# Second up product with stationary weights: both halves of all tokens move side by side, and three engines make the squared relu

## Chip, cores and metric

The kernel runs on one core of a Trainium2 chip. The metric is the device time of one execution in microseconds (us). TensorE multiplies, VectorE and ScalarE work on rows from its banks (PSUM) and from on-chip memory (SBUF), GpSimd works on SBUF, and the SyncE queue starts the loads from HBM. Every engine runs its own program strictly in order, and semaphores order the engines against one another.

## The reference, cut to what matters

256 tokens of width 1024 pass two blocks. The change lies in the last part of the second one, an MLP with a squared relu:

```python
u = rms_norm_2(x, g_mlp_pre) @ w_up        # 256 x 1024 @ 1024 x 4096
u = jnp.square(jax.nn.relu(u))
x = x + rms_norm_2(u @ w_down, g_mlp_post) # 256 x 4096 @ 4096 x 1024
```

## The kernel before

All large products are made from halves. ScalarE rounds an fp32 operand to the reduced type in which TensorE is fast (the high part), VectorE makes the rest (the low part, the operand less its high part), and TensorE adds up high x high, high x low and low x high in a bank (`three_products`, L1536 to L1541). Weights and activations are both split so.

The weights come in units of 128 x 2048 (1 MB), loaded by SyncE into eight places. `make_high` (ScalarE) and `make_low` (VectorE) split one unit each; there are four places for high parts, so a unit waits until the unit four before it is used up. In the up product `mu` the gain of the norm is folded into the weights, so that a unit is split in four pieces of 128 x 512 (L484, L504); the down product `md` splits a unit at once (L477, L495). ScalarE signals a unit once, behind its last piece, and VectorE starts on it then.

`mu` has 8 slabs of 512 of the 4096 columns, two units each (the first and the second 512 of the 1024 contracted values). For each slab, `split_use` makes 48 matmuls: the tokens are stationary, 128 by 128, and 512 columns of weights move through; the two tiles of 128 tokens have a bank each, and two slabs alternate between four banks `G`. The result has tokens on the partitions. ScalarE scales it by the norm's rstd, a column with one value for each token, and takes the relu (`relu`, L1473); VectorE squares it (`relu_squared`, L2979); TensorE turns the squares with transposes into banks `T` while it works on the slab behind (`squared_turn`); ScalarE copies the high part out of `T` (`hidden_high`, L1141) and VectorE makes the low part (`hidden_low`, L2352). So the squares stand with the 4096 values on the partitions, 32 chunks of 128, as `md` needs them for its stationary operand.

In each round s of the loop over slabs, ScalarE and VectorE first split the two units of slab s+1 (`make_slab`; in round 7 the first two of `md`), then take the turned squares of slab s-1, then scale and square slab s. `md` (`split_down`) has 16 units of two chunks. In its first unit it makes the products of one token tile, the last transposes, and then those of the other tile. `rest_high` and `rest_low` split its other units after the loop.

Of the kernel before, what the change touches and what calls it, by code (L numbers as in the profile page):

```python
# [16 lines left out]
P = 128  # L17
S = 256
# [197 lines left out]
def build(nc, t, out):  # L216
    with ExitStack() as ctx:
# [3 lines left out]
        def sem(name):  # L221
            return ctx.enter_context(nc.semaphore(name))
# [20 lines left out]
        dense_high = place(HIGH * UNIT, RAW * UNIT, "dense_high", F32R)  # L243
        xT_lo_all = place(KD * S, 12 * UNIT, "xT_lo_all", F32R)
        turned_all = place(4 * S, 13 * UNIT, "turned_all", F32)
        gate_parts_all = place(KD * 2 * HEADS + P, 13 * UNIT + 4 * S, "gate_parts_all", F32R)
# [69 lines left out]
        post_gain1 = work[:, 0, PROJ:PROJ + D]  # L316
        post_gain2 = ring[:, 6 * SLAB + KD * S:6 * SLAB + KD * S + D]

# [69 lines left out]
        sines_exp_ready = sem("sines_exp_ready")  # L388
        relu_ready = sem("relu_ready")
        relu2_ready = sem("relu2_ready")  # L390
# [39 lines left out]
        def consumed(eng, n):  # L430

            ph = phase_of(n)
            u = n - ph.first
            if ph in (ao, fo, bo, po, md):
                if u < ph.units - 1:
                    eng.wait_ge(ph.used, u + 1)
                else:
                    eng.wait_ge(down_full, ph.downs + 4)
            elif u % 2:
                eng.wait_ge(ph.full, 2 * (u // 2 + 1))  # L440
            else:
                eng.wait_ge(ph.half_used, u // 2 + 1)
# [415 lines left out]
        def _(pool):  # L858
# [169 lines left out]
            pool.wait_ge(rows_cleared, 1)  # L1028
            nc.gpsimd.memset(hT[0:AUG, 24:32, :], 0.0).then_inc(rows_cleared, 1)


        @block.scalar
        def _(act):
# [22 lines left out]

            def high_turn(tf, g, c, gc):

# [396 lines left out]
            post_norm_squares(12, 0)  # L1455
            high_turn(turned2, base, 0, None)
            post_norm_squares(12, 1, lambda: make_high(act, mu.first + 2))
            square(0, 16 + 2)
            high_turn(turned2, base + 2, 1, None)
            make_high(act, mu.first + 3)  # L1460
# [4 lines left out]

            def relu(s, c):
                n = 2 * s + c
                act.wait_ge(mu.full, n + 1)
                if s:
                    act.wait_ge(relu2_ready, n - 1)  # L1470
                else:
                    act.wait_ge(rstd_ready, 10 + c + 1)
                nc.scalar.activation(xn[:, c, 0:BANK], G[2 * (s % 2) + c][:, :], ACT.Relu, scale=rstd[:, c:c + 1]).then_inc(mu.done, 1)  # L1473

            for s in range(mu.slabs):
                if s:
                    make_slab(make_high, act, mu, s + 1, md)
                for c in range(NT):
                    if s:
                        hidden_high(turned2, base + 2 * (s - 1) + c, s - 1, c, 4)  # L1480
                for c in range(NT):
                    relu(s, c)
# [8 lines left out]
        def _(pe):  # L1491
# [56 lines left out]

            def split_first(ph, tc, base, other_tile, late=0):

# [657 lines left out]

            split_first(mu, tc, base, second_tile2, late=1)
            base += 4  # L2210
            for s in range(1, mu.slabs):
                split_use(mu, s, lambda: slab_before(squared_turn, s, base))
            pe.wait_ge(mu.done, 2 * mu.slabs - 2)

            def last_squared():
                pe.wait_ge(mu.done, 2 * mu.slabs)
                slab_before(squared_turn, mu.slabs, base)

            split_down(md, *hidden_parts, chunk_ready(base, 4, tc), last=4, free=mu.slabs % 2, turns=last_squared)


        @block.vector
        def _(dve):
# [51 lines left out]

            def low_turn(tc, c, gc, between=None):

# [684 lines left out]

            post_norm(1, post_gain1, 0)
            low_turn(tc, 0, None)
            make_low(dve, mu.first + 1)
            post_norm(1, post_gain1, 1)
            low_turn(tc, 1, None)
            make_low(dve, mu.first + 2)
# [4 lines left out]

            def relu_squared(s, c, base):
                n = 2 * s + c
                dve.wait_ge(mu.done, n + 1)
                if s:
                    dve.wait_ge(tf, base + n - 1)
                V.tensor_tensor(xn[:, c, BANK:2 * BANK], xn[:, c, 0:BANK], xn[:, c, 0:BANK], ALU.mult).then_inc(relu2_ready, 1)  # L2979

            for s in range(mu.slabs):
                if s:
                    make_slab(make_low, dve, mu, s + 1, md)
                for c in range(NT):
                    if s:
                        hidden_low(tc, s - 1, c, 4)
                for c in range(NT):
                    relu_squared(s, c, base)
            for c in range(NT):
                hidden_low(tc, mu.slabs - 1, c, 4)  # L2990
            rest_low(md)
# [25 lines left out]
```

## Time and profile before

| | |
|---|---|
| median of 3 runs | 1855.09 us (1854.59 to 1855.69) |
| profiled execution | 1854.42 us, span 1852.8 us |
| TensorE busy | 1837.0 us, 99% of the span |
| VectorE, ScalarE, GpSimd busy | 75%, 65%, 9% |
| chain that ended last | TensorE 96%, VectorE 2%, ScalarE 1% |
| slabs 1 to 7 of the up product | 1675.62 to 1758.13 us, 11.79 us each |

The span is the time from the first to the last recorded instruction; the 1.6 us between it and the device time lie around it. Matmuls are pipelined: each is shown with its whole duration, so they overlap in the record, and the pace is the distance between their starts.

### The profile page before, as it was taken

How to read it: one execution, taken by the hardware profiler on the slowest of the kernel's cores; microseconds unless marked ns; L12 is line 12 of the kernel's file. 1: busy time of each engine (PE TensorE's matmuls, PEld its weight loads, DVE VectorE, ACT ScalarE, POOL GpSimd, SP SyncE). 2: the span in 40 equal slices, each digit the busy share in tenths (PEclk: the TensorE clock that was granted, in tenths of full speed). 3: DMA queues.
4: the chain of work that ended last, by engine and by line, in shares of the span. 5: the costliest groups of instructions: out<-in, count | busy, mean ns of one | idle time of the engine just before them, and what ended most of it. 6: DMA issues, size and time to landing. Idle time of an engine off the chain costs nothing.

```text
span 1852.8 us, 25653 instructions
## 1 busy us (share of the span) xinstructions
PE 1837.0 (99%) x8824; PEld 1544.9 (83%) x8824; DVE 1394.9 (75%) x1561; ACT 1200.1 (65%) x1346; POOL 159.2 (9%) x185
## 2 busy tenths in 40 slices
PE   9999999999999999999999999999999999999998
PEld 8998888888888888888888888888888887878887
DVE  6666476646676888888888888988888997587653
ACT  5544365437765777677676777777777676666542
POOL 3000000004404400000000000000000321000000
PEclk9999999999999999999999999999999999999999
DMA  9656655554439999999999999999999973345550
GB/s 294 185 184 206 195 184 188 182 186 155 137 125 336 338 396 395 394 394 393 395 395 396 394 393 384 381 386 367 394 375 371 394 295 106 134 148 166 177 196 30
DMA packets 237863, 516.19 MB, mean 279 GB/s; under 512 B 15260, under 2 KB 55312, under 8 KB 237792
## 3 DMA queue, kind: packets, MB, share of 16 engines
q1 hardware_dynamic: 232304, 499.70, 75.3%
q0 software_dynamic: 5184, 14.51, 2.2%
q10 hardware_dynamic: 304, 1.05, 0.2%
q8 instruction: 41, 0.67, 0.1%
q14 instruction: 30, 0.25, 0.0%
HBM read 506.78 MB, written 8.42 MB: 278 GB/s over the span
## 4 chain that ended last, share of the span: by engine, by line
PE 96%; DVE 2%; ACT 1%; issue 0%; ACTq 0%; DVEq 0%; POOL 0%; POOLq 0%
PE G L1539 24%; PE G L1541 24%; PE G L1540 24%; PE SM L1541 5%; PE SM L1539 5%; PE SM L1540 5%; PE T L1499 3%; PE T L1952 1%; PE SM L1727 1%; PE G L1818 1%; DVE e_low L724 1%; PE SM L1836 0%; PE SM L2096 0%; PE G L1937 0%; PE G L2065 0%
## 5 line engine op out<-in xcount | busy, mean ns | idle before, releaser
L724 DVE TENSOR_TENSOR e_low<-e_arrived,e_high 128x2048 fp32r<-128x2048 f32 (+1 forms) x346 | 758.9, 2247 | 86.9 <-ACT e_high L716 86.9
L716 ACT CAST e_high<-e_arrived 128x2048 fp32r<-128x2048 f32 x338 | 624.4, 1914 | 4.8 <-PE SM L1541 4.8
L1539 PE MATMUL G<-e_high,work_r 128*128 128x512 f32 x896 | 353.8, 395 | 1.0 <-DVE e_low L724 0.7
L1541 PE MATMUL G<-e_high,work_r 128*128 128x512 f32 x896 | 349.4, 390 | 0.0
L1540 PE MATMUL G<-e_low,work_r 128*128 128x512 f32 x896 | 348.6, 389 | 0.0
L1539 PE MATMUL G<-dense_high,xT_hi_all 128*128 128x512 f32 (+1 forms) x760 | 294.2, 387 | 1.7 <-ACT work_all L1125 0.7
L1541 PE MATMUL G<-dense_high,xT_lo_all 128*128 128x512 f32 (+1 forms) x760 | 283.3, 373 | 0.0
L1540 PE MATMUL G<-dense_low,xT_hi_all 128*128 128x512 f32 (+1 forms) x760 | 282.5, 372 | 0.0
L495 DVE TENSOR_TENSOR dense_low<-dense_raw,dense_high 128x2048 fp32r<-128x2048 f32 (+1 forms) x73 | 147.9, 2055 | 89.1 <-ACT dense_high L477 88.1
L1541 PEld LDWEIGHTS G<-e_high,work_r 128*128 128x128 f32 x896 | 168.1, 188 | 35.9
L1539 PEld LDWEIGHTS G<-e_high,work_r 128*128 128x128 f32 x896 | 168.3, 188 | 35.2 <-DVE e_low L724 1.6
L1540 PEld LDWEIGHTS G<-e_low,work_r 128*128 128x128 f32 x896 | 168.4, 188 | 33.6
L504 DVE SCALAR_TENSOR_TENSOR dense_low<-dense_raw,gains,dense_high 128x512 fp32r<-128x512 f32 x216 | 148.7, 752 | 49.5 <-ACT dense_high L484 49.5
L1539 PE MATMUL SM<-e_high,work_r 128*128 128x512 f32 x448 | 175.8, 392 | 0.0
L477 ACT CAST dense_high<-dense_raw 128x2048 fp32r<-128x2048 f32 (+1 forms) x73 | 123.0, 1722 | 81.0 <-PE G L1541 81.0
L1541 PE MATMUL SM<-e_high,work_r 128*128 128x512 f32 x448 | 174.6, 390 | 0.0
L1540 PE MATMUL SM<-e_low,work_r 128*128 128x512 f32 x448 | 174.4, 389 | 0.0
L1539 PEld LDWEIGHTS G<-dense_high,xT_hi_all 128*128 128x128 f32 x760 | 143.0, 188 | 20.9 <-issue 1.6
L1541 PEld LDWEIGHTS G<-dense_high,xT_lo_all 128*128 128x128 f32 x760 | 142.6, 188 | 21.0
L1540 PEld LDWEIGHTS G<-dense_low,xT_hi_all 128*128 128x128 f32 x760 | 143.1, 188 | 17.9
L1539 PE MATMUL G<-dense_high,hT_hi_all 128*128 128x512 f32 x376 | 147.7, 393 | 0.8 <-ACT work_all L1219 0.8
L1540 PE MATMUL G<-dense_low,hT_hi_all 128*128 128x512 f32 x376 | 146.3, 389 | 0.0
(380 smaller groups left out, 2078.9 us busy)
## 6 DMA issues: line engine op xcount, KB each, us to landing
e_arrived<-in_m_w_in_dram SPq DMA_DIRECT2D x448, 512.0 KB, 8.6
e_arrived<-in_m_w_out_dram SPq DMA_DIRECT2D x224, 512.0 KB, 8.6
dense_raw<-in_a_w_in_dram SPq DMA_DIRECT2D x32, 768.0 KB, 6.0
dense_raw<-in_f_w_in_dram SPq DMA_DIRECT2D x44, 512.0 KB, 4.6
dense_raw<-in_w_up_dram SPq DMA_DIRECT2D x16, 1024.0 KB, 5.2
dense_raw<-in_w_down_dram SPq DMA_DIRECT2D x16, 1024.0 KB, 4.9
dense_raw<-in_a_w_out_dram SPq DMA_DIRECT2D x12, 1024.0 KB, 5.0
dense_raw<-in_f_w_out_dram SPq DMA_DIRECT2D x11, 1024.0 KB, 4.9
```

The source lines that it names most:

```text
L477: ins = nc.scalar.copy(high_place(n)[:, 0:4 * w], unit_place(n, dense_raw)[:, 0:4 * w])
L495: ins = nc.vector.tensor_tensor(unit_place(n, dense_low)[:, 0:4 * w], unit_place(n, dense_raw)[:, 0:4 * w], high_place(n)[:, 0:4 * w].bitc ...
L504: ins = nc.vector.scalar_tensor_tensor(out=low, in0=raw, scalar=by[kk], in1=high.bitcast(F32), op0=ALU.mult, op1=ALU.subtract)
L716: nc.scalar.copy(e_hi_unit(n), e_raw(n, e_arrived)).then_inc(e_hi, 1)
L724: ins = nc.vector.tensor_tensor(e_raw(n, e_low)[:, at], e_raw(n, e_arrived)[:, at], e_hi_unit(n)[:, at].bitcast(F32), ALU.subtract)
L1499: ins = nc.tensor.transpose(T[par(g)][0:k, at:at + P], src, ident[:, :])
L1539: nc.tensor.matmul(bank, x_hi, w_hi, start=start, stop=False)
L1540: nc.tensor.matmul(bank, x_hi, w_lo, start=False, stop=False)
L1541: return nc.tensor.matmul(bank, x_lo, w_hi, start=False, stop=stop)
L1727: nc.tensor.matmul(SM[c][:, 0:GDIM], work[:, c, A_HALF + s * P:A_HALF + (s + 1) * P], work[:, c, s * GDIM:(s + 1) * GDIM], start=True, sto ...
L1818: nc.tensor.matmul(G[2 + u % 2][:, 0:nk], hT[0:AUG, HEADS + hd, q * P:(q + 1) * P], hT[0:AUG, hd, 0:nk], start=True, stop=True).then_inc(a ...
L1952: ins = nc.tensor.transpose(T[p % 2][:, n * P:(n + 1) * P], e_hid[:, p % 2, n * P:(n + 1) * P], ident[:, :])
```

## The change

From its second slab on, the up product has the weights stationary. The halves of the activations of all 256 tokens lie side by side (`x_halves_all`, for each of the 8 contracted blocks 256 columns of high and 256 of low parts). With 128 x 128 of high weights stationary, one matmul moves all 512 columns into a bank: its left half gets high x high, its right half high x low. With the low weights stationary, a second matmul moves the 256 high columns and adds into the left half. A bank so holds 128 of the 4096 values for all 256 tokens, already with the values on the partitions; a slab fills four banks, and eight banks alternate. The transposes of slabs 1 to 7 go, and the relu's scale by rstd becomes a product with rows: one matmul of ones with a diagonal matrix of rstd spreads rstd over the partitions (`rstd_row`).

A chunk then passes three engines: ScalarE copies the right half out of the bank (`copy_side`), VectorE adds it to the left half (`sum_chunk`), GpSimd takes the relu and multiplies by `rstd_row`, ScalarE squares and makes the high part (`square_chunk`), and VectorE makes the low part (`lower_chunk`). Slab 0 stays as it was. `post_gain2`, the gain loaded on ScalarE's queue, has another place. The diff without declarations:

```diff
+            pool.wait_ge(side_ready, 3)
+            for m in range(4 * (mu.slabs - 1)):
+                pool.wait_ge(mu.done, 2 + m + 1)
+                steps.then(nc.gpsimd.tensor_scalar(up_sum[:, m % 4, :], up_sum[:, m % 4, :], 0.0, 1.0, ALU.max, ALU.mult))
+                nc.gpsimd.tensor_tensor(up_sum[:, m % 4, :], up_sum[:, m % 4, :], rstd_row, ALU.mult).then_inc(relu2_ready, 1)
...
+            def copy_side(m):
...
+                act.wait_ge(mu.full, 2 + m + 1)
+                if m >= 2:
+                    act.wait_ge(mu.done, 2 + m - 1)
+                nc.scalar.copy(up_side[:, m % 2, :], bank[:, S:2 * S]).then_inc(side_ready, 1)
+
+            def square_chunk(m):
+
+                act.wait_ge(relu2_ready, 2 + m + 1)
+                steps.then(nc.scalar.activation(up_square[:, m % 4, :], up_sum[:, m % 4, :], ACT.Square))
+                nc.scalar.copy(hT_hi[:, 4 + m, :], up_square[:, m % 4, :]).then_inc(split_copied, 1)
+
             for c in range(NT):
-                hidden_high(turned2, base + 2 * (mu.slabs - 1) + c, mu.slabs - 1, c, 4)
+                relu(c)
+            for s in range(1, mu.slabs):
+                make_slab(make_high, act, mu, s + 1, md)
+                if s == 1:
+                    for c in range(NT):
+                        hidden_high(turned2, base + c, 0, c, 4)
+                    act.wait_ge(side_ready, 2)
+                    nc.scalar.copy(rstd_row, G[0][:, 0:S]).then_inc(side_ready, 1)
+                for j in range(4):
+                    m = 4 * (s - 1) + j
+                    copy_side(m)
+                    if m:
+                        square_chunk(m - 1)
+            square_chunk(4 * (mu.slabs - 1) - 1)
...
+            def up_slab(s, between):
+
+                banks = up_banks(s)
+                for part in range(2):
+                    n = mu.first + 2 * s + part
+                    split_ready(n)
+                    w_hi, w_lo = high_place(n), low_place(n)
+                    for j in range(4):
...
+                        elif part == 0 and s > 2:
+                            pe.wait_ge(mu.done, 2 + 4 * (s - 3) + j + 1)
+                        for kk in range(4):
+                            k = 4 * part + kk
+                            at = slice(kk * BANK + j * P, kk * BANK + (j + 1) * P)
+                            both = lambda stop: nc.tensor.matmul(banks[j][:, :], w_hi[:, at], x_halves_all[:, 2 * k * S:2 * (k + 1) * S],
+                                                                 start=(k == 0), stop=stop)
+                            if k < KD - 1:
+                                both(False)
+                            ins = nc.tensor.matmul(banks[j][:, 0:S], w_lo[:, at], mu_hi[:, k, :], start=False, stop=False)
+                            if k == KD - 1:
+                                ins = both(True)
+                        if part:
+                            ins.then_inc(mu.full, 1)
...
+            def first_squared():
+
+                slab_before(squared_turn, 1, base)
+                pe.wait_ge(side_ready, 1)
+                nc.tensor.matmul(G[0][:, 0:S], ones[:, :], rstd_diag, start=True, stop=True).then_inc(side_ready, 1)
...
+            pe.wait_ge(mu.done, 2 + 4 * (mu.slabs - 2))
+
+            def last_free():
+                pe.wait_ge(mu.done, 2 + 4 * (mu.slabs - 2) + 2)
...
+            split_down(md, *hidden_parts, up_ready, last=4, free=0, turns=last_free)
...
+            for c in range(NT):
+                ins = V.tensor_scalar(rstd_diag[:, c * P:(c + 1) * P], ident[:, :], rstd[:, c:c + 1], None, ALU.mult)
+            ins.then_inc(side_ready, 1)
...
+            def sum_chunk(m):
...
+                dve.wait_ge(side_ready, 3 + m + 1)
+                V.tensor_tensor(up_sum[:, j, :], bank[:, 0:S], up_side[:, m % 2, :], ALU.add).then_inc(mu.done, 1)
+
+            def lower_chunk(m):
+
+                high_parts[0] += 1
+                dve.wait_ge(split_copied, high_parts[0])
+                V.tensor_tensor(hT_lo[:, 4 + m, :], up_square[:, m % 4, :], hT_hi[:, 4 + m, :].bitcast(F32), ALU.subtract
+                                ).then_inc(tc[0], 1)
+
             for c in range(NT):
-                hidden_low(tc, mu.slabs - 1, c, 4)
+                relu_squared(c)
+            for s in range(1, mu.slabs):
+                make_slab(make_low, dve, mu, s + 1, md)
+                if s == 1:
+                    for c in range(NT):
+                        hidden_low(tc, 0, c, 4)
+                for j in range(4):
+                    m = 4 * (s - 1) + j
+                    if m >= 2:
+                        lower_chunk(m - 2)
+                    sum_chunk(m)
+            for m in (4 * (mu.slabs - 1) - 2, 4 * (mu.slabs - 1) - 1):
+                lower_chunk(m)
```

## Rows read from the trace of the kernel before

**Rows 1.** Page, 40 slices of the span: granted TensorE clock in tenths.

```profile
PEclk9999999999999999999999999999999999999999
```

**Rows 2.** Waits of TensorE, 1660 us to the end.

```profile
PE G L1539 <- DVE xT_lo_all L2286: 0.2, 1, 0.2
```

**Rows 3.** Windows of slabs 1 and 7: busy us (instructions), clock, DMA share, GB/s.

```profile
1675.62:1687.40 11.78, 11.78 (x57) 9.84 (x56) 9.12 (x22) 8.22 (x15) 0.00 (x0) 1.00 0.70 246
...
1746.34:1758.13 11.79, 11.79 (x58) 9.84 (x57) 7.07 (x6) 6.06 (x6) 0.00 (x0) 1.00 0.49 180
```

**Rows 4.** Timeline of TensorE in slab 3: start us, us, operation, tiles, count.

```profile
1699.64 0.39 PE L1541 MATMUL G<-dense_high,xT_lo_all 128*128 128x512 f32 x1
...
1704.40 0.39 PE L1541 MATMUL G<-dense_high,xT_lo_all 128*128 128x512 f32 x1
1704.64 1.03 PE L1499 MATMUL T<-ident,xn_all 128*128 128x128 f32 x8
```

**Rows 5.** Timeline of TensorE, 256-wide matmuls among 512-wide ones.

```profile
424.11 0.28 PE L1784 MATMUL SM<-xT_hi_all,gate_parts_all 128*128 128x256 f32 x1
424.22 0.29 PE L1784 MATMUL SM<-xT_lo_all,gate_parts_all 128*128 128x256 f32 x1
424.34 0.28 PE L1784 MATMUL SM<-xT_hi_all,gate_parts_all 128*128 128x256 f32 x1
...
426.48 0.28 PE L1784 MATMUL SM<-xT_hi_all,gate_parts_all 128*128 128x256 f32 x1
```

**Rows 6.** One line's instructions (L1784): duration ns min/median/max, first and last start.

```profile
L1784 PEld LDWEIGHTS SM<-xT_hi_all,gate_parts_all x16: 186/188/190, 423.9 to 1548.3; 128*128 128x128 f32 x16
```

**Rows 7.** Groups by form, TensorE: plain fp32 matmul.

```profile
L1727 PE MATMUL SM<-work_all 128*128 128x384 f32 x32 | 11.6, 486 | 0.0
```

**Rows 8.** Groups by form, ScalarE.

```profile
L482 ACT CAST dense_high<-dense_raw 128x512 fp32r<-128x512 f32 x64 | 36.5, 619 | 0.2 <-issue 0.2
...
L1242 ACT COPY turned_all<-T 128x256 f32<-128x256 f32 x16 | 6.0, 374 | 9.8 <-PE T L1499 9.8
...
L1404 ACT ACTIVATE xn_all<-work_all 128x128 f32<-128x128 f32 x8 | 2.4, 304 | 0.0
```

**Rows 9.** Groups by form, VectorE.

```profile
L2352 DVE TENSOR_TENSOR work_r<-T,hT_hi_all 128x256 fp32r<-128x256 f32 x22 | 8.2, 415 | 2.4 <-ACT hT_hi_all L1141 2.4
```

**Rows 10.** Timeline of VectorE, up product and start of the down product.

```profile
1681.50 5.39 DVE L504 SCALAR_TENSOR_TENSOR dense_low<-dense_raw,gains,dense_high 128x512 fp32r<-128x512 f32 x8 [1.75 <-ACT dense_high L484]
1686.81 1.28 DVE L2352 TENSOR_TENSOR work_r<-T,hT_hi_all 128x512 fp32r<-128x512 f32 x2
...
1749.06 4.49 DVE L495 TENSOR_TENSOR dense_low<-dense_raw,dense_high 128x2048 fp32r<-128x2048 f32 x2 [1.10 <-ACT dense_high L477]
```

**Rows 11.** Timeline of GpSimd.

```profile
430.02 0.20 POOL L920 TENSOR_TENSOR stats<-stats 128x8 f32<-128x8 f32 x1
430.30 1.05 POOL L923 TENSOR_TENSOR work_all<-work_all,stats 128x512 f32<-128x512 f32 x1
```

**Rows 12.** Groups by form, GpSimd.

```profile
L988 POOL TENSOR_SCALAR work_r<-work_all,stats 128x256 fp32r<-128x256 f32 x1 | 0.9, 945 | 5.9 <-DMA work_all<-last_slots 5.9
...
L869 POOL TENSOR_SCALAR_AFFINE_SELECT causal<-causal 128x256 f32<-128x256 f32 x1 | 0.4, 402 | 0.1
```

**Rows 13.** Timeline of GpSimd, beside VectorE's subtractions.

```profile
1435.01 2.27 POOL L1024 TENSOR_TENSOR h_all<-h_all,xn_all 128x512 f32<-128x512 f32 x1 [7.11 <-DMA xn_all<-y_table]
```

**Rows 14.** Timeline of ScalarE, up product and start of the down product.

```profile
1678.92 5.01 ACT L484 ACTIVATE dense_high<-dense_raw,gains 128x512 fp32r<-128x512 f32 x8
1683.83 1.05 ACT L1141 CAST hT_hi_all<-T 128x512 fp32r<-128x512 f32 x2
...
1747.12 3.71 ACT L477 CAST dense_high<-dense_raw 128x2048 fp32r<-128x2048 f32 x2
```

**Rows 15.** Timeline of VectorE, beside the GpSimd addition.

```profile
1433.83 10.00 DVE L724 TENSOR_TENSOR e_low<-e_arrived,e_high 128x2048 fp32r<-128x2048 f32 x4 [0.46 <-ACT e_high L716]
```

**Rows 16.** Page, costliest groups.

```profile
L724 DVE TENSOR_TENSOR e_low<-e_arrived,e_high 128x2048 fp32r<-128x2048 f32 (+1 forms) x346 | 758.9, 2247 | 86.9 <-ACT e_high L716 86.9
```

More of the change, by code:

```diff
@@ L439, in consumed @@
             elif u % 2:
-                eng.wait_ge(ph.full, 2 * (u // 2 + 1))
+                eng.wait_ge(ph.full, 2 + 4 * (u // 2) if ph is mu else 2 * (u // 2 + 1))
             else:
@@ L1464, in _ @@
             base += 4
[L1466 to L1482, printed above, removed]
@@ L1483, in _, with relu @@
-            for c in range(NT):
-                hidden_high(turned2, base + 2 * (mu.slabs - 1) + c, mu.slabs - 1, c, 4)
+            def relu(c):
+                act.wait_ge(mu.full, c + 1)
+                act.wait_ge(rstd_ready, 10 + c + 1)
+                nc.scalar.activation(xn[:, c, 0:BANK], G[c][:, :], ACT.Relu, scale=rstd[:, c:c + 1]).then_inc(mu.done, 1)
+            def copy_side(m):
+                s, j = 1 + m // 4, m % 4
+                bank = ((G[2], G[3], SM[0], SM[1]) if s % 2 else (T[0], T[1], G[0], G[1]))[j]
+                act.wait_ge(mu.full, 2 + m + 1)
+                if m >= 2:
+                    act.wait_ge(mu.done, 2 + m - 1)
+                nc.scalar.copy(up_side[:, m % 2, :], bank[:, S:2 * S]).then_inc(side_ready, 1)
@@ L1547, in split_ready, with split_first @@
                     pe.wait_ge(dense_lo, split_count(n))
-            def split_first(ph, tc, base, other_tile, late=0):
+            def split_first(ph, tc, base, other_tile, late=0, xT_hi=xT_hi, xT_lo=xT_lo):
                 for c in range(NT):
@@ L2207, in second_tile2, with up_banks @@
                 keep_busy(SM[0], 8)
-            split_first(mu, tc, base, second_tile2, late=1)
+            def up_banks(s):
+                return (G[2], G[3], SM[0], SM[1]) if s % 2 else (T[0], T[1], G[0], G[1])
+            def up_slab(s, between):
[5 more added lines that the diff above has]
+                    for j in range(4):
+                        if part == 0 and s == 2:
+                            pe.wait_ge(tc[j % 2], base // 2 + 1)
+                            pe.wait_ge(mu.done, 2)
+                            pe.wait_ge(side_ready, 3)
+                        elif part == 0 and s > 2:
[12 more added lines that the diff above has]
+                            ins.then_inc(mu.full, 1)
+                    if part == 0:
+                        ins.then_inc(mu.half_used, 1)
+                        between()
@@ L2215, in last_squared, with up_ready @@
[L2215 to L2219, printed above, removed]
+                up_slab(s, first_squared if s == 1 else lambda: None)
+            pe.wait_ge(mu.done, 2 + 4 * (mu.slabs - 2))
+            def last_free():
+                pe.wait_ge(mu.done, 2 + 4 * (mu.slabs - 2) + 2)
+            def up_ready(k):
+                if k == 0:
+                    for c in range(NT):
+                        pe.wait_ge(tc[c], base // 2 + 1)
+                elif k >= 4:
+                    pe.wait_ge(tc[0], base // 2 + 1 + (k - 4) + 1)
@@ L2274, in norm_rstd, with low_turn @@
                 norm_scale(c)
-            def low_turn(tc, c, gc, between=None):
+            def low_turn(tc, c, gc, between=None, xT_hi=xT_hi, xT_lo=xT_lo):
                 for j in range(2):
@@ L2972, in _, with relu_squared @@
             base += 4
[L2974 to L2978, printed above, removed]
[L2979 to L2990 removed]
+            for c in range(NT):
+                ins = V.tensor_scalar(rstd_diag[:, c * P:(c + 1) * P], ident[:, :], rstd[:, c:c + 1], None, ALU.mult)
+            ins.then_inc(side_ready, 1)
+            def relu_squared(c):
+                dve.wait_ge(mu.done, c + 1)
+                V.tensor_tensor(xn[:, c, BANK:2 * BANK], xn[:, c, 0:BANK], xn[:, c, 0:BANK], ALU.mult).then_inc(relu2_ready, 1)
+            def sum_chunk(m):
+                s, j = 1 + m // 4, m % 4
+                bank = ((G[2], G[3], SM[0], SM[1]) if s % 2 else (T[0], T[1], G[0], G[1]))[j]
+                dve.wait_ge(side_ready, 3 + m + 1)
[5 more added lines that the diff above has]
+                                ).then_inc(tc[0], 1)
+            for c in range(NT):
+                relu_squared(c)
+            for s in range(1, mu.slabs):
+                make_slab(make_low, dve, mu, s + 1, md)
+                if s == 1:
+                    for c in range(NT):
+                        hidden_low(tc, 0, c, 4)
[6 more added lines that the diff above has]
+                lower_chunk(m)
             rest_low(md)
```

24 lines of the change are left out of this document (15 added, 9 removed).

## Prediction

> **What bounds the kernel now.** I read the slices of the page first: TensorE's granted clock is full in all 40 [rows 1]. Then the waits of TensorE from 1660 us to the end: one wait of 0.2 us in 193 us [rows 2]. So the second MLP runs at TensorE's own pace, and here the change must be judged by what it does to TensorE's stream and by whether the other engines can still stay ahead of it. The windows give the pace: the seven slabs 1 to 7 of the up product take 11.79 us each, with VectorE busy 7.1 to 9.1 us and ScalarE 6.1 to 8.2 us of it, and GpSimd not at all [rows 3]. The timeline splits the 11.79 us: from the matmul at 1699.64 to that at 1704.40 there are 21 steps, 4.76/21 = 0.227 us each, so 48 matmuls of 512 columns are 10.88 us [rows 4]. The other 0.90 us is the group of eight transposes, whose 1.03 us overlaps the next product [rows 4]. The reader is to see that ScalarE and VectorE are idle a quarter to a half of the time, but that they work in a fixed order: high parts of the next slab, low parts behind them, then the previous slab's results.
>
> **What the change removes and adds on TensorE.** The transposes of slabs 1 to 7 go: 7 x 0.90 = 6.3 us. The products keep their columns: per slab 32 matmuls of 512 and 32 of 256 instead of 48 of 512, so 16 instructions and weight loads more. A 256-wide matmul with its own load stands in the trace: between 424.11 and 426.48 lie two rounds of four of 256 and three of 512 [rows 5]; 2.37 - 6 x 0.227 = 1.01, or 0.126 us each, though each load takes 0.19 us [rows 6]: loads are hidden. Inside a run of such matmuls the step is 0.12 us. A pair of 512 and 256 is thus 0.353 us (0.345 at best), a slab 32 x 0.353 = 11.3 us (11.0). The one product that spreads rstd over the partitions is plain fp32, 256 wide; the nearest row, 384 wide, is 0.49 us [rows 7]: taken as 0.5. TensorE alone would then gain 6.3 - 7 x (11.3 - 10.88) - 0.5 = 2.9 us, at best 4.8.
>
> **What it adds beside TensorE.** Per slab, four chunks each pass ScalarE (copy of one half), VectorE (sum), GpSimd (relu, then scale), ScalarE (square, then high part), VectorE (low part). Prices:
> ScalarE's copy of 256 columns from PSUM is 0.37 us [rows 8]; square and cast of 256 from SBUF lie between 0.30 (128) and 0.62 (512) [rows 8], 0.41 each, and with the wait between them a pair is 0.85.
> VectorE's 256-wide subtraction is 0.42 us [rows 9], and 0.34 behind another, since two of 0.68 take 1.28 [rows 10]; sum and low part are of that form.
> GpSimd: a two-input operation of 8 elements is 0.20 us and one of 512 is 1.05 [rows 11], so 256 cost 0.62. For the one-input relu there are 0.94 us (a 256-wide tensor_scalar, once) and 0.40 (a 256-wide select) [rows 12]; I take 0.70, between them. With 0.1 to wake, 0.08 between and 0.05 to the next engine, a chunk holds GpSimd 1.55 us; the bounds are 1.25 and 1.88 (0.94 for the relu, and 0.70 for the scale from a slower row: 2.27 us for 512, of which some 1.07 went by until VectorE's running operation ended [rows 13]).
> By the cycles per element that the Trainium skill gives (GPSIMD Engine Reference, Elementwise), two-input 256 would be about 0.70 us and one-input 0.54, an estimate; the sum below would be 1.2 us less. No row here shows a one-input operation of this size free of doubt.
>
> As busy time this fits: VectorE 5.4 + 8 x 0.37 = 8.4, ScalarE 5.0 + 4 x 0.27 + 4 x 0.75 = 9.1, GpSimd 6.2 of 11.3 us. But the queues are in order, and the order closes a loop. In round s ScalarE makes the high parts of slab s+1, then for j = 0..3 copies chunk j and squares chunk j-1. It cannot copy chunk 2 before it has squared chunk 0, and that waits for GpSimd, which waits for the sum of chunk 0, and VectorE reaches that sum only behind the eight low parts of the same round, which wait for ScalarE's high parts. And ScalarE starts the next round's high parts only behind the square of chunk 2. Let X be the start of a round's high parts:
> - low parts start at X + 2.58 (1678.92 to 1681.50), the next VectorE operation 5.31 later (1686.81) [rows 10, 14]: X + 7.89.
> - low part of an old chunk 0.34, sum of chunk 0 0.42: X + 8.65.
> - GpSimd 1.55; square and high part 0.85; VectorE's wake and low part of chunk 0 0.39; sum of chunk 2 0.42; GpSimd 1.55; square and high part of chunk 2 0.75 to the next issue: 5.51.
> - The low part of chunk 0 comes due while GpSimd works on chunk 1. Whether they get in each other's way: four VectorE subtractions took 10.00 us where 4 x 2.25 = 9.0 [rows 15, 16] is their sum, while one GpSimd addition ran [rows 13], so VectorE lost 1.0 us. I add 0.2, from bounds of 0 and one GpSimd operation, 0.7.
> Period 8.65 + 5.71 = 14.36 us, against the 11.3 that TensorE needs. The bounds are 13.56 (relu 0.40, no clash) and 15.5 (relu 0.94, 0.70, clash 0.7). So **TensorE waits some 3 us for the low parts of every slab**, and this is the cost of the change.
>
> **The sum.** The first round starts as before, X1 = 1678.92 [rows 14]; the two high and low parts of slab 0 stay in it, its VectorE work ends at 1686.81 + 1.28 = 1688.1 [rows 10], the sum of chunk 0 at 1688.5, so X2 = 1688.5 + 5.71 = 1694.2. Slabs 2 and 3 still find their weights in time or nearly; from then on TensorE follows at X + 5.3, when the first unit's four low parts are made. X7 = 1694.2 + 5 x 14.36 = 1766.0. In that round the weights are those of the down product: high parts 3.71 us for two, low parts 4.49 [rows 10, 14]. Half of each, 1.9 and 2.25, is one unit: the first is ready at X7 + 4.15 = 1770.2; twelve products (2.72 us) later the second token tile needs banks that the second sum of slab 7 frees at X7 + 1.9 + 4.49 + 2 x 0.76 = 1773.9. In the profile of before, the same point lies at 1758.13 + 2.72 + 0.90 = 1761.75 [rows 3, 4]: 12.15 us later. The third unit of the down product is the last thing late: ScalarE reaches it after the square of the last chunk, 1.6 us (the next GpSimd turn) behind that of the chunk before: X7 + 7.15 + 5.71 + 1.6 = 1780.5. It is ready 4.15 later, at 1784.65, and TensorE arrives at 1773.9 + 2.72 + 5.44 = 1782.05: 2.6 us more. Behind it each unit costs ScalarE 1.9 and VectorE 2.25 us against TensorE's 24 x 0.227 = 5.44, so nothing more is lost or won back. In all +14.8 us. The 2.9 us won on TensorE is in this, as idle time of TensorE. The vector copy of rstd's diagonal (two small operations) and the moved gain load are covered: the first by some 2 us until the transposes of slab 0 are over and the product needs its result, the second by the whole up product.
> The profiled execution took 1854.42 us (span 1852.8), the median of the runs is 1855.09; 1854.4 + 14.8 = 1869.2 and by the median **1869.9 us**. With the bounds of the period the sum is +9.2 and +22.8: 1864 and 1878.
>
> **Rivals.**
> 1. GpSimd and VectorE block each other wherever both have SBUF inputs: the upper bounds at once, 1878 us. For it: the 1.0 us lost at 1433.83 [rows 15]; against it: the sums read a PSUM bank and only one SBUF operand, and during the low parts GpSimd has mostly finished. The Trainium skill (SBUF — State Buffer, Who interferes with whom) states that a VectorE instruction with two SBUF inputs and a GpSimd one that reads SBUF exclude each other for a whole instruction; by that rule the low parts of chunks 0 and 1 wait each time. The trace agrees with its lost 1.0 us. Chance 0.17.
> 2. Not slower: the loop closes within TensorE's slab, and only TensorE's stream counts: 1855.1 - 2.9 = 1852.2, at best 1850.3. It decides once the period is 11.3 or less, that is once the tail of 5.71 us shrinks to 2.65. For it: the busy sums fit. Against it: the ScalarE and VectorE steps in that tail are 2.4 us by rows, so GpSimd's two turns would have to cost 0.1 us each. Chance 0.09.
> 3. The granted clock falls in TensorE's new idle times. Only stalls of up to a few tenths of a us stand in the MLP of before, at full clock [rows 1, 2], so nothing here shows it. Up to 3 us per slab would vanish in the wait; with a whole slab at 1.2 GHz (22.6 us) the time would be near 1855 + 6 x (22.6 - 11.79) = 1920. Chance 0.04.
>
> **How the numbers follow.** My case, with its bounds, 0.67; the three rivals 0.17, 0.09, 0.04; 0.03 for a GpSimd quicker than its bound (a period of 12.8 us would still be +4). Faster and slower are counted from 0.2% (3.7 us), about what a measurement of this kernel can tell from no change. Slower: 0.67 + 0.17 + 0.04 + 0.02 = 0.90. Rival 2 straddles the line: 0.04 faster, 0.05 same, and 0.01 more same. The range takes in both bounds with some room for relu's price, and leaves rivals 2 and 3 out: 1861 to 1879.
>
> **What the new profile would show.** Right: TensorE waiting about 3 us in front of slabs 4 to 7, ended by VectorE's low parts; rounds of ScalarE's eight high parts 14.4 us apart; ScalarE's squares waiting for GpSimd; a pair of matmuls every 0.35 us. Wrong, if the rounds stand 11.3 us apart, if GpSimd's two operations together are far from 1.3 us, or if the clock row shows less than 9 there.

## The result, and the profile after

The changed kernel takes 1879.23 us (median of 4 runs, 1878.65 to 1879.73) against 1854.97 us: a ratio of 1.0131, with the interval 1.0119 to 1.0143. It is 24.3 us slower; 14.8 were predicted, and the time lies 0.2 us above the upper end of the range. The profiled execution of the change took 1879.12 us, 24.7 more than that of before.

The waits of TensorE from 1660 us to the end, in the change (total, times, longest; before there was one of 0.2 us, [rows 2]):

```profile
PE T L2259 <- DVE dense_low L511: 7.8, 2, 3.9
PE G L2259 <- DVE dense_low L511: 5.6, 3, 2.4
PE G L1568 <- DVE dense_low L502: 3.8, 1, 3.8
PE G L1568 <- issue: 2.8, 1, 2.8
PE G L1568 <- DVE xn_all L3063: 0.5, 1, 0.5
...
```

TensorE now waits in front of the slabs, each time for VectorE's low parts of the weights (L511, before L504), and in front of the units of the down product (L502, before L495). The 2.8 us that the view puts down to "issue" lie in front of the first of those units. The rounds of ScalarE show the period; its timeline, the rows in which a round's high parts begin:

```profile
1679.43 5.00 ACT L491 ACTIVATE dense_high<-dense_raw,gains 128x512 fp32r<-128x512 f32 x8
...
1695.71 5.01 ACT L491 ACTIVATE dense_high<-dense_raw,gains 128x512 fp32r<-128x512 f32 x8
...
1711.13 5.00 ACT L491 ACTIVATE dense_high<-dense_raw,gains 128x512 fp32r<-128x512 f32 x8
...
1726.55 5.01 ACT L491 ACTIVATE dense_high<-dense_raw,gains 128x512 fp32r<-128x512 f32 x8
...
1772.83 3.70 ACT L484 CAST dense_high<-dense_raw 128x2048 fp32r<-128x2048 f32 x2
```

From 1695.71 to 1772.83 there are five rounds of 15.42 us; before, the rounds followed TensorE's 11.79 us [rows 3, 14]. Inside one round, GpSimd's timeline (the rows that answer to [rows 11, 12]):

```profile
1704.45 1.17 POOL L1040 TENSOR_SCALAR xn_all<-xn_all 128x256 f32<-128x256 f32 x1 [7.68 <-DVE xn_all L3063]
1705.70 0.74 POOL L1041 TENSOR_TENSOR xn_all<-xn_all,xT_all 128x256 f32<-128x256 f32 x1
1706.41 1.07 POOL L1040 TENSOR_SCALAR xn_all<-xn_all 128x256 f32<-128x256 f32 x1
1707.56 0.82 POOL L1041 TENSOR_TENSOR xn_all<-xn_all,xT_all 128x256 f32<-128x256 f32 x1
1708.35 1.07 POOL L1040 TENSOR_SCALAR xn_all<-xn_all 128x256 f32<-128x256 f32 x1
1709.50 0.83 POOL L1041 TENSOR_TENSOR xn_all<-xn_all,xT_all 128x256 f32<-128x256 f32 x1
1710.30 1.07 POOL L1040 TENSOR_SCALAR xn_all<-xn_all 128x256 f32<-128x256 f32 x1
```

A chunk's turn is relu plus scaling, 1.95 us, and the turns of chunks 0 to 2 follow one another with no wait for VectorE, from 1704.45 to 1710.33. Behind them, ScalarE's timeline (the idle time ahead of an operation in brackets):

```profile
1710.37 0.42 ACT L1496 ACTIVATE xn_all<-xn_all 128x256 f32<-128x256 f32 x1 [0.82 <-POOL xn_all L1041]
1710.82 0.41 ACT L1497 CAST hT_hi_all<-xn_all 128x256 fp32r<-128x256 f32 x1
1711.13 5.00 ACT L491 ACTIVATE dense_high<-dense_raw,gains 128x512 fp32r<-128x512 f32 x8
```

Then VectorE's, the sum of chunk 0, the low part of chunk 0, the sum of chunk 2, and the low parts of the next slab:

```profile
1703.94 0.42 DVE L3063 TENSOR_TENSOR xn_all<-T,xT_all 128x256 f32<-128x256 f32 x1
...
1707.36 0.43 DVE L3069 TENSOR_TENSOR work_r<-xn_all,hT_hi_all 128x256 fp32r<-128x256 f32 x1 [2.33 <-ACT hT_hi_all L1497]
1707.71 0.42 DVE L3063 TENSOR_TENSOR xn_all<-G,xT_all 128x256 f32<-128x256 f32 x1
...
1713.72 5.39 DVE L511 SCALAR_TENSOR_TENSOR dense_low<-dense_raw,gains,dense_high 128x512 fp32r<-128x512 f32 x8 [3.65 <-ACT dense_high L491]
```

The sum of chunk 2 ends at 1708.13, and GpSimd takes chunk 2 up only at 1708.35, when it has finished chunk 1. So three GpSimd turns in a row lie on the loop, and the steps of ScalarE and VectorE between them are hidden behind GpSimd.

The windows (busy time and count of TensorE, weight loads, VectorE, ScalarE, GpSimd; then clock, DMA share, GB/s), which answer to [rows 3]:

```profile
1700.00:1716.00 16.00, 11.74 (x65) 9.80 (x64) 8.84 (x18) 9.77 (x22) 7.40 (x8) 1.00 0.54 169
1716.00:1732.00 16.00, 13.13 (x65) 11.14 (x65) 8.82 (x18) 9.76 (x23) 7.42 (x8) 0.89 0.33 111
...
1747.00:1763.00 16.00, 13.30 (x65) 11.27 (x66) 8.82 (x18) 9.77 (x23) 7.41 (x8) 0.89 0.29 104
...
1778.00:1794.00 16.00, 11.74 (x49) 9.00 (x48) 8.39 (x13) 9.10 (x13) 7.50 (x8) 0.96 0.40 147
1794.00:1810.00 16.00, 16.00 (x67) 13.11 (x66) 10.06 (x5) 5.76 (x4) 0.00 (x0) 0.93 0.38 131
```

The page's row of the clock reads 9 throughout, as before [rows 1]; its slices of 47 us are too coarse. The windows show 0.89 twice in the up product and 0.93 to 0.96 around the start of the down product. TensorE's timeline at the down product's third unit:

```profile
1788.76 0.39 PE L1570 MATMUL G<-dense_high,work_r 128*128 128x512 f32 x1
1792.92 0.79 PE L1568 MATMUL G<-dense_high,hT_hi_all 128*128 128x512 f32 x1 [3.78 <-DVE dense_low L502]
1793.52 0.63 PE L1569 MATMUL G<-dense_low,hT_hi_all 128*128 128x512 f32 x1
1793.94 0.63 PE L1570 MATMUL G<-dense_high,work_r 128*128 128x512 f32 x1
...
1796.37 0.39 PE L1570 MATMUL G<-dense_high,work_r 128*128 128x512 f32 x1
```

Behind the wait, a matmul of 512 columns comes every 0.43 us and not every 0.23: TensorE runs at 1.2 GHz until 1796.4 (granted clock 0.52 from 1792.9 to 1796.3) and at 2.4 GHz behind that (1.00).

### The profile page after: what moved, and what is told of

The parts are those of the page before. It is cut to its first block, busy times and chain, and to the rows that moved or that the text cites. A ratio compares the mean times of both kernels' runs of the same rounds, so it can differ in the third digit from the quotient of the medians.

```text
span 1877.5 us, 25907 instructions
## 1 busy us (share of the span) xinstructions
PE 1841.5 (98%) x8882; PEld 1548.8 (82%) x8882; DVE 1397.7 (74%) x1591; ACT 1213.2 (65%) x1403; POOL 212.8 (11%) x241
## 4 chain that ended last, share of the span: by engine, by line
PE 89%; DVE 5%; ACT 2%; POOL 2%; issue 1%; ACTq 0%; POOLq 0%; DVEq 0%
PE G L1568 22%; PE G L1570 22%; PE G L1569 22%; PE SM L1570 5%; PE SM L1568 5%; PE SM L1569 5%; PE T L1528 3%; DVE dense_low L511 2%; PE T L1981 1%; POOL xn_all L1040 1%; POOL xn_all L1041 1%; ACT dense_high L491 1%; DVE e_low L731 1%; PE SM L1756 1%; DVE dense_low L502 1%
## 5 line engine op out<-in xcount | busy, mean ns | idle before, releaser
L1568 PE MATMUL G<-dense_high,xT_hi_all 128*128 128x512 f32 (+1 forms) x632 | 243.7, 386 | 1.5 <-ACT work_all L1137 0.7
L1570 PE MATMUL G<-dense_high,xT_lo_all 128*128 128x512 f32 (+1 forms) x632 | 233.4, 369 | 0.0
L1569 PE MATMUL G<-dense_low,xT_hi_all 128*128 128x512 f32 (+1 forms) x632 | 232.6, 368 | 0.0
L502 DVE TENSOR_TENSOR dense_low<-dense_raw,dense_high 128x2048 fp32r<-128x2048 f32 (+1 forms) x73 | 147.9, 2056 | 90.2 <-ACT dense_high L484 89.0
L511 DVE SCALAR_TENSOR_TENSOR dense_low<-dense_raw,gains,dense_high 128x512 fp32r<-128x512 f32 x216 | 148.7, 753 | 59.1 <-ACT dense_high L491 59.0
L491 ACT ACTIVATE dense_high<-dense_raw,gains 128x512 fp32r<-128x512 f32 x216 | 137.2, 714 | 12.8 <-PE G L1570 12.8
L1319 ACT CAST work_r<-T 128x512 fp32r<-128x512 f32 x56 | 32.9, 587 | 154.7 <-PE T L1981 154.7
L1570 PEld LDWEIGHTS G<-dense_high,xT_lo_all 128*128 128x128 f32 x632 | 118.6, 188 | 16.0
```

What stands on the lines that cost most here:

```text
L491: ins = nc.scalar.mul(high_place(n)[:, at], unit_place(n, dense_raw)[:, at], by[kk])
L502: ins = nc.vector.tensor_tensor(unit_place(n, dense_low)[:, 0:4 * w], unit_place(n, dense_raw)[:, 0:4 * w], high_place(n)[:, 0:4 * w].bitc ...
L511: ins = nc.vector.scalar_tensor_tensor(out=low, in0=raw, scalar=by[kk], in1=high.bitcast(F32), op0=ALU.mult, op1=ALU.subtract)
L1319: nc.scalar.copy(e_hT_hi[:, p % 2, :], T[p % 2][:, :]).then_inc(e_turned_hi, 1)
L1568: nc.tensor.matmul(bank, x_hi, w_hi, start=start, stop=False)
L1569: nc.tensor.matmul(bank, x_hi, w_lo, start=False, stop=False)
```

## Experiments

**Theory A** (the prediction's): ScalarE, VectorE and GpSimd, each in order, close a loop that is longer than TensorE's slab, and GpSimd's turns lie on it. **Theory B**: VectorE and GpSimd exclude each other, and that sets the pace. **Theory C**: TensorE's own stream or its clock is what costs.

**1. The relu left out.**

```diff
-                steps.then(nc.gpsimd.tensor_scalar(up_sum[:, m % 4, :], up_sum[:, m % 4, :], 0.0, 1.0, ALU.max, ALU.mult))
```

> GpSimd's relu is left out (its scale by rstd stays), so the output is that of an MLP without relu. Theory A (a closed loop of in-order queues, two GpSimd turns in each round): a turn shrinks from 2.1 to 0.9 us, the rounds from 15.4 to about 12.8 us, the time from 1879 to about 1860 us. Theory B (VectorE and GpSimd exclude each other at SBUF, and that sets the pace): half of GpSimd's work is gone, VectorE's two-input operations get shorter by what they lost, total between 1865 and 1875. Theory C (TensorE's new stream is slow by itself, or its clock): rounds stay near 15.4 us, 1877 to 1880.

Measured: 1858.84 us, ratio 1.0024 (1.0015 to 1.0033); rounds 12.88 us. Removing 1.07 us of GpSimd work from each chunk shortens a round by 2.54 us and the whole by 20.4 us: GpSimd's time is on the path. Here GpSimd waits for the sum of chunk 2, which the change's GpSimd does not:

```profile
1716.28 0.42 DVE L3062 TENSOR_TENSOR xn_all<-SM,xT_all 128x256 f32<-128x256 f32 x1
1716.78 0.74 POOL L1040 TENSOR_TENSOR xn_all<-xn_all,xT_all 128x256 f32<-128x256 f32 x1 [1.07 <-DVE xn_all L3062]
```

**2. Relu and scale in one VectorE operation, GpSimd idle.**

```diff
-                steps.then(nc.gpsimd.tensor_scalar(up_sum[:, m % 4, :], up_sum[:, m % 4, :], 0.0, 1.0, ALU.max, ALU.mult))
-                nc.gpsimd.tensor_tensor(up_sum[:, m % 4, :], up_sum[:, m % 4, :], rstd_row, ALU.mult).then_inc(relu2_ready, 1)
...
+                dve.wait_ge(mu.done, 2 + m + 1)
+                V.scalar_tensor_tensor(out=up_sum[:, j, :], in0=up_sum[:, j, :], scalar=0.0, in1=rstd_row,
+                                       op0=ALU.max, op1=ALU.mult).then_inc(relu2_ready, 1)
```

> Relu and scale are one VectorE operation of 0.42 us behind each sum; GpSimd does nothing here. Theory A: the loop remains by its order, eight low parts, then sum, square, low part, sum, square; rounds of about 12.2 us, still more than the 11.3 us of TensorE's stream, total near 1858 us. Theory B: no clash is left, so TensorE alone sets the pace: 1851 to 1853 us. Theory C: 1877 to 1880.

Measured: 1854.16 us, ratio 0.9998 (0.9988 to 1.0007); rounds 12.17 us. The period came as expected, the time 4 us lower than expected: TensorE's waits there are only 0.9, 0.6, 0.3 and 0.2 us. It is no faster than before although the transposes are gone; its loop is still longer than TensorE's slab of 11.3 us. Why TensorE waits so little stays open.

**3. Two weight pieces behind each chunk, and squares and low parts one chunk later.** The same operations on the same engines; eight pieces in a block become four pairs. The block for slab 2 moves ahead of the loop (not shown in the cut), so the weights are also made one slab earlier than in the change.

```diff
                     copy_side(m)
-                    if m:
-                        square_chunk(m - 1)
+                    if m >= 2:
+                        square_chunk(m - 2)
+                    if s + 2 <= mu.slabs:
+                        make_high(act, mu.first + 2 * (s + 2) + j // 2, (2 * (j % 2), 2 * (j % 2) + 1))
...
-                    if m >= 2:
-                        lower_chunk(m - 2)
+                    if m >= 3:
+                        lower_chunk(m - 3)
                     sum_chunk(m)
+                    u = 2 * (s + 2) + (j // 2 - 1)
+                    if 6 <= u <= 2 * mu.slabs + 1:
+                        make_low(dve, mu.first + u, (2 * (j % 2), 2 * (j % 2) + 1))
```

> All operations stay on their engines; only the order changes: ScalarE and VectorE take two pieces of the next weights behind each chunk instead of eight in a block ahead of four chunks, and square and low part come one chunk later. Theory A: no loop is left that is longer than TensorE's slab, so the rounds are 11.0 to 11.3 us and the time is 1850 to 1853 us, slightly below the kernel before. Theory B: GpSimd's operations now fall beside VectorE's low parts all the time, so their durations grow by several tenths of a us and the rounds stay above 12.5 us, total above 1862. Theory C: 1877 to 1880.

Measured: 1852.03 us, ratio 0.9986 (0.9976 to 0.9995). TensorE's waits, all of them from 1660 us on:

```profile
PE G L1570 <- DVE x_halves_all L2363: 0.2, 1, 0.2
```

GpSimd's groups by form there:

```profile
L1040 POOL TENSOR_SCALAR xn_all<-xn_all 128x256 f32<-128x256 f32 x28 | 40.6, 1449 | 141.0 <-DVE xn_all L3065 141.0
L1041 POOL TENSOR_TENSOR xn_all<-xn_all,xT_all 128x256 f32<-128x256 f32 x28 | 22.6, 805 | 2.3
```

The relu costs 1.45 us here against 1.09 in the change, so GpSimd and VectorE hinder each other more, and still 27.2 us are gone. Theory B falls as the cause, though its mechanism is there. Theory C falls for the stream: the same matmuls run without a wait.

**4. The relu made twice.**

```diff
                 steps.then(nc.gpsimd.tensor_scalar(up_sum[:, m % 4, :], up_sum[:, m % 4, :], 0.0, 1.0, ALU.max, ALU.mult))
+                steps.then(nc.gpsimd.tensor_scalar(up_sum[:, m % 4, :], up_sum[:, m % 4, :], 0.0, 1.0, ALU.max, ALU.mult))
```

> GpSimd takes the relu twice (the second changes nothing). Theory A: 1.15 us more per turn, two turns per round, so the rounds go from 15.4 to about 17.8 us and the time to about 1879 + 6 x 2.4 + 3.5 = 1897 us. Theory B: the same work on GpSimd finds VectorE mostly idle, so some 3 to 8 us more. Theory C: no change.

Measured: 1905.64 us, ratio 1.0273 (1.0257 to 1.0289); the starts of two of its rounds:

```profile
1718.28 5.00 ACT L491 ACTIVATE dense_high<-dense_raw,gains 128x512 fp32r<-128x512 f32 x8
1737.14 5.00 ACT L491 ACTIVATE dense_high<-dense_raw,gains 128x512 fp32r<-128x512 f32 x8
```

Rounds of 18.86 us, 3.44 more than the change. The second relu takes 1.07 to 1.16 us: three of it, not two. This miss of the expectation showed that three GpSimd turns lie on the loop.

**5. Only the squares later, weight pieces still in a block.**

```diff
-                    if m:
-                        square_chunk(m - 1)
+                    if m >= 2:
+                        square_chunk(m - 2)
...
-                    if m >= 2:
-                        lower_chunk(m - 2)
+                    if m >= 3:
+                        lower_chunk(m - 3)
```

> The weight blocks of a round stay as in the change (eight high parts, then four chunks); only the squares come one chunk later (chunk m-2 behind the copy of chunk m) and the low parts too (m-3). Theory A (a closed loop of in-order queues; three GpSimd turns of 1.97 us lie on it): ScalarE is back at the next high parts behind the square of chunk 1 and not of chunk 2, so one turn leaves the loop: rounds 15.42 - 1.97 = 13.45 us, time 1879 - 6 x 1.97 = 1867, and about 1866 if part of the clock's loss goes too. Theory B (VectorE and GpSimd excluding each other set the pace): the same operations overlap in the same places, so rounds stay near 15.4 and the time near 1879. Theory C (TensorE's stream and clock): 1879.

Measured: 1868.98 us, ratio 1.0077 (1.0059 to 1.0095); rounds 13.61 us, 1.81 less: one turn leaves the loop. The eight low parts take 5.53 us, not 5.39, as they begin while GpSimd still scales the round's last chunk; this 0.14 us is about what the round is over 13.45.

**6. Only the weight pieces spread, squares as in the change.**

```diff
                     if m:
                         square_chunk(m - 1)
+                    if s + 2 <= mu.slabs:
+                        make_high(act, mu.first + 2 * (s + 2) + j // 2, (2 * (j % 2), 2 * (j % 2) + 1))
```

(The low parts likewise behind each sum, and the block for slab 2 ahead of the loop as in experiment 3.)

> Two weight pieces behind each chunk, as in the version with both edits, but the square stays one chunk behind the copy, as in the change. Theory A: the wait for GpSimd is then paid once for each chunk, but GpSimd works while ScalarE and VectorE make weights; the chain of one chunk (copy 0.37, sum 0.42, GpSimd 1.9 to 2.2, square and high part 0.83, two weight pieces 1.25) is about 3.0 us less what overlaps, so a slab is near TensorE's 11.3 and at most 12.5: 1852 to 1858 us. If the later square were what had cured the version with both edits, this one would stay near 1866 or above. Theory B: weight work now overlaps GpSimd's everywhere, so more than 1879. Theory C: 1879.

Measured: 1851.58 us, ratio 0.9983 (0.9973 to 0.9993), the best of all. Its window over the up product:

```profile
1676.00:1760.00 84.00, 84.00 (x476) 73.05 (x475) 65.86 (x127) 65.21 (x144) 58.95 (x55) 1.00 0.57 194
```

TensorE is busy throughout at full clock. The block of eight pieces in each queue is what makes the loop long: GpSimd had nothing to do for the 7.7 us in which ScalarE and VectorE made weights (the bracket at 1704.45 above), and they waited for GpSimd behind it. Spread, the two kinds of work overlap. That the weights come a slab earlier is not what cured it, since the loop itself is now shorter than TensorE's slab. ScalarE's timeline, the same pair of pieces in two rounds:

```profile
1707.61 1.33 ACT L491 ACTIVATE dense_high<-dense_raw,gains 128x512 fp32r<-128x512 f32 x2
...
1718.11 1.34 ACT L491 ACTIVATE dense_high<-dense_raw,gains 128x512 fp32r<-128x512 f32 x2
```

A round takes 10.50 us, with no wait of ScalarE for TensorE in it. The later square adds nothing to this (experiment 3).

**7. TensorE kept busy in the last stall.** In front of the third unit of the down product:

```diff
+                    if ph is md and u == 2:
+                        keep_busy(T[1], 33)
```

> The change as it is, with 33 transposes of no use (4.0 us of TensorE at their usual pace) in the stall in front of the down product's third unit. If the matmuls behind that stall run at the lower granted clock because TensorE stood still, the stretch behind it is at full clock now (512 columns every 0.227 us) and the time falls by 1.3 to 1.8 us, to about 1877.6. If the lower clock has another cause, or costs nothing, 1879.2.

Measured: 1877.34 us, ratio 1.0122 (1.0104 to 1.0141), 1.9 us below the change. TensorE's timeline:

```profile
1789.20 3.76 PE L1683 MATMUL T<-ident 128*128 128x128 f32 x33
1793.14 0.50 PE L1568 MATMUL G<-dense_high,hT_hi_all 128*128 128x512 f32 x1 [0.18 <-DVE dense_low L502]
1793.48 0.40 PE L1569 MATMUL G<-dense_low,hT_hi_all 128*128 128x512 f32 x1
1793.72 0.39 PE L1570 MATMUL G<-dense_high,work_r 128*128 128x512 f32 x1
```

The matmuls behind the stall are at full clock now (granted 1.00 from 1793.1 to 1796.5, 0.52 in the change). The third unit begins 0.2 us later than in the change, as its first round did already (1679.63 for 1679.43), and yet the profiled span is 1.4 us shorter. So the lower clock costs 1.6 us by the traces and 1.9 by the medians, whose runs spread over 0.5 and 1.1 us; and its cause is that TensorE stood still.

**8. A relu of one operation.**

```diff
-                steps.then(nc.gpsimd.tensor_scalar(up_sum[:, m % 4, :], up_sum[:, m % 4, :], 0.0, 1.0, ALU.max, ALU.mult))
+                steps.then(nc.gpsimd.tensor_scalar(up_sum[:, m % 4, :], up_sum[:, m % 4, :], 0.0, None, ALU.max))
```

> GpSimd's relu with one arithmetic operation (max with 0) and not two (max, then times 1.0). If the 1.07 us of the relu comes from its second operation, it falls to about 0.6 or 0.7; by theory A three turns on the loop then save 3 x 0.4 = 1.2 us a round: rounds 14.2 us, time about 1871. If the price is that of a one-input operation whatever it computes, 1.07 us, rounds 15.4 and 1879 stay.

Measured: 1876.97 us, ratio 1.0119 (1.0101 to 1.0137); rounds 15.31 us. Neither expectation: the relu fell to 0.85 us, but the round only by 0.10. GpSimd's timeline, chunks 1 and 2:

```profile
1706.16 0.84 POOL L1040 TENSOR_SCALAR xn_all<-xn_all 128x256 f32<-128x256 f32 x1
1707.09 0.74 POOL L1041 TENSOR_TENSOR xn_all<-xn_all,xT_all 128x256 f32<-128x256 f32 x1
1708.53 0.85 POOL L1040 TENSOR_SCALAR xn_all<-xn_all 128x256 f32<-128x256 f32 x1 [0.70 <-DVE xn_all L3063]
```

and VectorE's beside it:

```profile
1707.12 0.99 DVE L3069 TENSOR_TENSOR work_r<-xn_all,hT_hi_all 128x256 fp32r<-128x256 f32 x1 [2.11 <-ACT hT_hi_all L1497]
1708.03 0.41 DVE L3063 TENSOR_TENSOR xn_all<-G,xT_all 128x256 f32<-128x256 f32 x1
```

With the shorter relu, the low part of chunk 0 starts 0.03 us behind GpSimd's scaling (in the change it came 0.2 us ahead of it) and takes 0.99 us, not 0.43; the sum of chunk 2 comes late and GpSimd stands idle 0.70 us. What the relu gives, the clash takes. This holds for the profiled execution, 1878.14 us: the four runs fall into two pairs, near 1878.0 and near 1876.0, and no trace shows the faster pair. Experiments 9 and 10 bear on this reading.

**9. The sum ahead of the low part.**

```diff
-                    if m >= 2:
-                        lower_chunk(m - 2)
                     sum_chunk(m)
+                    if m >= 2:
+                        lower_chunk(m - 2)
```

> The change with VectorE's two steps for a chunk exchanged: first the sum of chunk m, then the low part of chunk m-2. Theory A: the old chunk's low part (0.34 us) leaves the loop in front of the sum of chunk 0; the three GpSimd turns behind it stay as they are (they run back to back already), so rounds fall from 15.42 to about 15.1 us and the time from 1879.2 to about 1877. Theory B (exclusion of VectorE and GpSimd sets the pace): the same pairs of operations still meet, no fall. Theory C: 1879.

Measured: 1876.81 us, ratio 1.0117 (1.0100 to 1.0134); rounds 15.08 us, 0.34 less, as expected.

**10. Both.** The edits of 8 and 9 together.

> Both: GpSimd's relu with one operation (0.85 us and not 1.07) and the sum ahead of the low part. With the one operation alone the rounds fell by 0.10 us only, because the low part of chunk 0 then fell on GpSimd's scaling (0.99 us and not 0.43) and held up the sum of chunk 2, so that GpSimd stood idle 0.7 us. If that is the cause, here the sum no longer waits for it: GpSimd's three turns of about 1.64 us run back to back, rounds 15.1 - 3 x 0.3 = 14.2 us, about 1872 us. If GpSimd's turns are not on the loop after all, or VectorE's steps are held up elsewhere as much, rounds 15.0 and 1877 as with the exchange alone.

Measured: 1871.04 us, ratio 1.0089 (1.0073 to 1.0106); rounds 14.46 us. With the sum first, the shorter relu is worth 0.62 us a round where alone it was worth 0.10: GpSimd's turns, now 1.74 us, follow one another again (at most 0.1 us between them), and three times 0.21 is 0.63. By the medians it is worth 5.8 us here (1876.81 to 1871.04) and 2.3 alone (1879.23 to 1876.97). So the clash ate most of the gain in 8. The round is 0.26 over the 14.2 expected, since a turn is 1.74 us and not 1.64: three of the round's four relus take 0.95 to 1.03.

## Why the prediction was wrong, step by step

The direction, the mechanism and the place were right in the main: a loop of in-order queues longer than TensorE's slab, TensorE waiting for the low parts (L511, then L502), ScalarE's squares waiting for GpSimd. **The step that failed is the tail of the loop behind the sum of chunk 0**, priced at 5.71 us: it measures 6.77 (1704.36 to 1711.13). What stands ahead of it, 8.65 us, was exact (1695.71 to 1704.36). A second term, the clock behind TensorE's stalls, stood in the sum with nothing and cost some 1.7 us.

- **GpSimd's turn, 1.55 us, was too cheap.** It is 1.95: the relu 1.07 (0.70 taken; even the bound of 0.94 was too low), the scaling 0.74 to 0.83 (0.62 taken, bound 0.70). The relu took 1.07 with VectorE idle beside it (1710.30), so this is its own price and no clash. One operation fewer in it saves 0.22 us (experiment 8).
- **Because of that, the path changed form.** The prediction walked two turns with a square, a low part and a sum between them: 0.85 + 0.39 + 0.42 = 1.66 us. Once a turn is longer than 1.66, chunk 2 finds GpSimd still at chunk 1, and the path is three turns end to end. Experiment 4 gives the count: 3.44 us for a second relu of 1.07 to 1.16. Experiment 1 shows the predicted form: without the relu a turn is under 1.66, GpSimd waits for the sum of chunk 2, and the tail of 4.23 us (1714.09 to 1718.32) is two turns of about 0.9 with the steps between them.
- **The clash of 0.2 us** was not paid at VectorE in the change (the low part took 0.43), only at GpSimd's scaling (0.83 for 0.74). A slightly other timing makes it 0.56 (experiment 8), inside the bounds of 0 and 0.7.

The measured tail still lies just inside the upper bound (15.5 - 8.65 = 6.85), but by luck: the bound gets there with a clash of 0.7 us that was hardly paid, and not with a third turn.

The sum by these: the point where the third unit of the down product starts was put at 1784.65 us and lies at 1792.92. Of the 8.3 us, 0.5 are there before the first round (1679.43 for 1678.92; over the profiled runs of this document it starts between 1678.86 and 1679.69, so this is spread between executions), 1.0 come in the first round, 5 x 1.06 = 5.3 in the five behind it, and 1.4 in the last (its tail, and one more turn of 1.95 for 1.6). To these come some 1.7 us at the lower clock. 14.8 + 8.3 + 1.7 = 24.8, and the profiled executions differ by 24.7. Without the 1.7 us of the clock the time would have been about 1877.5, inside the range: the mis-sized tail took the time near the upper end, and the clock took it past.

**What held.** The pair of 512 and 256 columns, in the timeline of experiment 3:

```profile
1688.99 0.40 PE L2261 MATMUL T<-x_halves_all,dense_high 128*128 128x512 f32 x1
1689.22 0.28 PE L2265 MATMUL T<-x_halves_all,dense_low 128*128 128x256 f32 x1
...
1690.76 0.40 PE L2261 MATMUL T<-x_halves_all,dense_high 128*128 128x512 f32 x1
```

Five pairs in 1.77 us, 0.354 each (0.353 from [rows 5]). TensorE alone was to gain 2.9 us: without the waits the kernel is 3.0 us faster than before (1851.58 against 1854.62, experiment 6). Copy 0.37, square 0.42, cast 0.41, sum and low part 0.42 us came as priced [rows 8, 9]; the second tile of the first down unit started 7.82 us behind its round, 7.9 predicted.

**The rivals.** Rival 1, mutual blocking, named a time near the one measured (1878), but not for its reason: in the change the low parts run at 0.42 us on average, and where blocking is strongest (experiments 3 and 6) the kernel is fastest. The mechanism is real: in experiment 8, VectorE's low part begins 0.03 us behind GpSimd's scaling and ends 0.28 us behind its end, about as if it had waited for it. By the Trainium skill (SBUF — State Buffer, Who interferes with whom), a VectorE instruction with two SBUF inputs contends with a GpSimd one that reads SBUF, and the one that comes second waits. The trace agrees there. Where the low part comes first the loss is smaller: in the change it had 0.23 us left when GpSimd's scaling began (1707.56), which lost 0.08 (0.82 for 0.74). Rival 2 is what the kernel does once the order is mended: 1852.2 was named, 1851.58 measured. Rival 3, the clock, came true in small. The stretches at 1.2 GHz in the up product lie inside what the loop leaves TensorE to wait. The rows where two slabs begin behind a wait show it:

```profile
1716.51 0.50 PE L2259 MATMUL T<-x_halves_all,dense_high 128*128 128x512 f32 x1 [3.86 <-DVE dense_low L511]
...
1731.94 0.50 PE L2259 MATMUL G<-x_halves_all,dense_high 128*128 128x512 f32 x1 [2.35 <-DVE dense_low L511]
```

The slab from 1716.51 has such a stretch (0.50 granted from 1717.7 to 1720.8), and the wait behind it is 2.35 us, where 3.86 stood before and 3.90 stands behind the next slab, which ran at full clock; the slabs begin 15.4 us apart all the same. Only the stretch behind the last stall shows in the time, 1.6 to 1.9 us by experiment 7.

Left open is why the relu with two operations takes 1.07 us where the scaling, with two inputs, takes 0.74.

## What to carry to other kernels

When work is handed to a third engine, write down for each in-order queue what stands ahead of the handover and behind its return: here the engines' busy sums all fitted into 11.3 us, and a block of eight weight pieces in two queues made 15.4 of it. Spreading such a block between the handovers, without changing any operation, took 27.7 us off. And price a chain of unequal stations by its slowest one too: once its turn is longer than the way round through the others, every item counts in full.

## What was not expected of the hardware

- On 128x256 fp32, GpSimd's tensor_scalar took 1.07 us with two operations (max, multiply) and 0.84 with one, while a two-input tensor_tensor took 0.74: the form with one input is the slower. By the cycles per element of the Trainium skill (GPSIMD Engine Reference, 3.1 Elementwise), a best case of 1.8 and about 2.6 for two inputs, and with some 0.15 us for the instruction itself, the prediction's estimates were 0.54 for one input and 0.70 for two; the trace agrees on the second and not on the first.
- VectorE's scalar_tensor_tensor and GpSimd's relu hinder each other as well. In experiment 6 the relu at 1709.74 takes 1.50 us beside two such operations that began at 1709.57; 1.07 alone.
- The granted clock fell for a few microseconds behind stalls of TensorE, out of sight of the page's slices. In the change's up product, matmuls behind a wait of 3.86 us (1716.51) began at full clock, a pair every 0.35 us, and went over to 0.64 us a pair from 1717.67 to 1720.85 (granted clock 1.00 from 1716.5 to 1717.6, 0.50 from 1717.7 to 1720.8).
